# A second pair of input tiles issued ahead of four small parameter loads, and two tiles turned before the parameters' rows

## The reference, cut to what matters

```python
h = rms_norm(x, mix_norm)                  # x * rsqrt(mean(x*x) + 1e-6) * mix_norm
proj = h @ w_in                            # 1024 x 1184
c_q, c_kv, k_pe, u_ssm, conv_a, conv_g = split(proj)
# three mixers: latent attention, a diagonal state-space model (S5), a gated convolution
dt = exp(log_dt); lam_bar = exp((lam_re + 1j * lam_im) * dt)     # parameters of the S5 mixer
x = x + concat(norm(y_attn), norm(y_ssm), norm(y_conv)) @ w_out
x = x + mixture_of_experts(rms_norm(x, ffn_norm))                # 32 experts, two for each token
```

## Time and profile before

| | us |
|---|---|
| runs without a profile, median of 3 | 1185.68 (1184.81 to 1186.89) |
| the profiled execution, its own time | 1187.53 |
| span of that execution in the trace | 1185.8 |
| TensorE busy | 1125.4 (95% of the span) |
| VectorE busy | 978.6 (83%) |
| ScalarE busy | 704.8 (59%) |
| GpSimd busy | 359.7 (30%) |
| mean DMA rate | 220 GB/s |

### The profile page before, as it was taken

How to read it: one execution, slowest core, us unless ns; L and a number is a source line. 1 busy time by engine, 2 the same in 40 slices (tenths; PEclk the granted TensorE clock), 3 DMA queues, 4 the chain that set the end, 5 groups by cost and what they waited for, 6 DMA issues and landing times.

```text
span 1185.8 us, 16012 instructions
## 1 busy us (share of the span) xinstructions
PE 1125.4 (95%) x5762; PEld 873.7 (74%) x5762; DVE 978.6 (83%) x1205; ACT 704.8 (59%) x825; POOL 359.7 (30%) x350
## 2 busy tenths in 40 slices
PE   5999999789999799998899999999999999999996
PEld 3457465666676577888788888888888888888885
DVE  5999989766657654367999999999999999999993
ACT  6521226755466541223577777777777777777772
POOL 4231012379970000112222333323333223223321
PEclk9999999899999899998999999999999999999998
DMA  8300010000005012236999999999999999999962
GB/s 278 111 1 1 1 25 5 1 1 2 2 20 230 1 36 75 86 128 239 382 369 374 374 396 385 389 399 382 395 383 386 389 367 371 393 375 370 397 231 55
DMA packets 40840, 260.96 MB, mean 220 GB/s; under 512 B 16366, under 2 KB 17114, under 8 KB 26970
## 3 DMA queue, kind: packets, MB, share of 16 engines
q1 hardware_dynamic: 30698, 243.03, 52.2%
q0 software_dynamic: 10096, 17.34, 6.0%
HBM read 252.26 MB, written 26.35 MB: 235 GB/s over the span
## 4 chain that ended last, share of the span: by engine, by line
PE 82%; DVE 10%; ACT 3%; issue 3%; DMA 1%; POOL 0%; POOLq 0%; SPq 0%; DVEq 0%; ACTq 0%
PE psum L2243 31%; PE psum L2263 15%; PE psum L1852 8%; PE psum L2151 7%; PE psum L2061 4%; PE psum L2091 3%; DVE arena L1144 3%; PE psum L1905 3%; PE psum L2233 2%; PE psum L2079 2%; PE psum L2249 1%; DVE am L1498 1%; DVE w_rest L1673 1%; PE psum L2047 1%; DMA arena<-in_x 1%
## 5 line engine op out<-in xcount | busy, mean ns | idle before, releaser
L1673 DVE TENSOR_TENSOR w_rest<-w,w_high 128x2048 fp32r<-128x2048 f32 x136 | 305.2, 2286 | 18.7 <-ACT w_high L1056 17.0
L1056 ACT ACTIVATE w_high<-w 128x2048 fp32r<-128x2048 f32 x136 | 256.2, 1913 | 45.4 <-PE psum L2243 42.0
L2243 PE MATMUL psum<-w_high,xgT_high 128*128 128x512 f32 x544 | 216.1, 397 | 3.0 <-DVE xgT_rest L1718 3.0
L2243 PE MATMUL psum<-w_rest,xgT_high 128*128 128x512 f32 x544 | 213.4, 392 | 0.0
L2243 PE MATMUL psum<-w_high,xgT_rest 128*128 128x512 f32 x544 | 212.7, 391 | 0.0
L1725 DVE TENSOR_TENSOR w_rest<-w,w_high 128x2048 fp32r<-128x2048 f32 x66 | 148.1, 2286 | 0.0
L691 POOL DMA_INDIRECT out<-arena,idx x34 | 91.3, 2687 | 106.8 <-DVE arena L1738 101.4
L1066 ACT ACTIVATE w_high<-w 128x2048 fp32r<-128x2048 f32 x66 | 122.4, 1906 | 0.0
L2243 PEld LDWEIGHTS psum<-w_high,xgT_high 128*128 128x128 f32 x544 | 102.7, 189 | 23.7 <-issue 2.2
L2243 PEld LDWEIGHTS psum<-w_rest,xgT_high 128*128 128x128 f32 x544 | 102.5, 188 | 22.0
L2243 PEld LDWEIGHTS psum<-w_high,xgT_rest 128*128 128x128 f32 x544 | 102.7, 189 | 20.5
(11 more groups left out here) (303 smaller groups left out, 2055.2 us busy)
## 6 DMA issues: line engine op xcount, KB each, us to landing
w<-in_w SPq DMA_DIRECT2D x102, 2048.0 KB, 10.3
arena<-in_x SPq DMA_DIRECT2D x5, 1024.0 KB, 9.2
h_scratch<-arena SPq DMA_DIRECT2D x8, 512.0 KB, 2.7
out<-arena SPq DMA_DIRECT2D x8, 512.0 KB, 3.6
arena<-in_x SPq DMA_DIRECT2D x1, 3072.0 KB, 19.1
arena<-in_w_in SPq DMA_DIRECT2D x1, 2688.0 KB, 12.1
arena<-in_w_in SPq DMA_DIRECT2D x1, 2048.0 KB, 13.8
wout_y_raw<-in_w_out SPq DMA_DIRECT2D x1, 2048.0 KB, 7.9
```

Of the source, the lines that this page charges most:

```text
L1056: act.activation(w13h[k][:, c, :], w13[b][k][:, c, :], ACT.Copy).then_inc(W13H_READY[k], 1)
L1673: dve.tensor_tensor(w13l[b][k][:, c, :], w13[b][k][:, c, :], w13h[k][:, c, :].bitcast(F32), S_).then_inc(W13_SPLIT[k], 1)
L2243: last = pe.matmul(psum[:, k, :], x_[:, c, :], w_[:, c, :], start=(c == 0 and n == 0), stop=(c == KC - 1 and n == 2))
```

## The change

On SP's queue `load_x(1)` moves ahead of the four small loads. On VectorE `scale_x(0)` and `scale_x(1)` move ahead of the wait for the transposed parameters and of the two copies; the short steps keep their order, and `scale_x(2)` and `scale_x(3)` keep their places among them. On TensorE `turn_x` takes the tiles' range instead of a half, tiles 0 and 1 are turned before the wait for the four small loads, and tiles 2 and 3 after the parameters' transpose. The number of instructions, their shapes, and the buffers stay as they are.

```diff
@@ SP
             load_x(0)
+            load_x(1)
             for k, lam in enumerate((lam_re, lam_im)):
                 sp.dma_start(first_rows[k * NPAIR:(k + 1) * NPAIR, :], lam[0].rearrange("(r h) s -> r (h s)", h=2)).then_inc(first_rows_in, 16)
...
                 sp.dma_start(ldt.rearrange("p r h -> p (r h)"), log_dt[0].partition_broadcast(P)).then_inc(first_rows_in, 16)
-            load_x(1)
@@ VectorE
+            scale_x(0)
+            scale_x(1)
             dve.wait_ge(hi_filled, R_P1 + 1)
             link(dve.tensor_copy(lamc[:, 0:2, :], psum[:, 5, 0:2 * NPAIR].rearrange("p (k r) -> p k r", k=2)))
             link(dve.tensor_copy(normc[:, 0:KC], psum[:, 5, 2 * NPAIR:2 * NPAIR + KC]))
             dve.sem_inc(hi_drained, 1)
             lr, li = lamc[:, 0, :], lamc[:, 1, :]
-            scale_x(0)
             for h in range(2):
                 ts(v(0)[h * S:(h + 1) * S, :], ldt[h * S:(h + 1) * S, :, h], 1.0 / 16, None, M_)
             ts(v(1), v(0), 1.0 / 9, 1.0, M_, A_)
-            scale_x(1)
             exp_terms(8, 6)
             scale_x(2)
@@ TensorE
-            def turn_x(half):
-                for i in range(4 * half, 4 * half + 4):
+            def turn_x(i0, i1):
+                for i in range(i0, i1):
...
+            turn_x(0, 2)
             pe.wait_ge(first_rows_in, 16 * 4)
             n = 2 * NPAIR + KC
             pe.transpose(psum[:, 5, 0:n], first_rows[:, :], ident[0:n, 0:n]).then_inc(hi_filled, 1)
...
             for half in range(2):
-                turn_x(half)
+                turn_x(4 * half + (0, 2)[half == 0], 4 * half + 4)
```

## The result

| | kernel before | changed kernel |
|---|---|---|
| median of 16 runs, us | 1185.16 (1183.30 to 1186.89) | 1187.59 (1184.79 to 1191.89) |
| profiled execution, its own time | 1187.53 | 1188.29 |
| its span | 1185.8 | 1186.5 |

The ratio is 1.0021 (95% interval 1.0013 to 1.0028): the change costs 2.4 us, 0.21%. The forecast was 1186.4 us, 0.7 us above the median of 1185.68 that was known then, and 0.89 for a difference too small to tell. (The ratios in this document are not the quotients of the medians beside them, and lie up to 0.0013 from these.)

A forecast was written before the change was run, and what follows sets the result against it. The prediction took TensorE's chain through the first projection's start at 18.79 as the bound. Terms of -0.14 (queue and VectorE's list) and +0.84 (clock) made +0.7 on a median of 1185.68: 1186.4 us, range 1183.8 to 1187.6.

The forecast's parts named there:

- What bounds the kernel: TensorE's chain: whatever moves the first projection's start at 18.79 moves the end by the same amount.
- Second pair at 8.11: SP's queue: x's second pair of tiles, loaded ahead of the small loads, lands at 8.11 instead of 11.91.
- The small loads' stall of 3.80 us carried over unchanged: SP's queue: the four small loads land 3.80 us behind x's second pair, at 11.91 instead of 9.51.
- the first rival: Small loads' stall shrinks behind x's second pair: half gives 1184.0 us, chance 0.10; gone gives 1183.1, chance 0.05.
- Tiles 0 and 1 hidden: TensorE's 16 transposes of tiles 0 and 1 end near 12.1, in idle time, as the parameters land.
- -0.14: VectorE's list: starting at 12.22, it begins scale_x(3) at 15.97, 0.14 us earlier than 16.11.
- The clock: TensorE: a 3 us gap ahead of tile 2 leaves the lower clock level, so its transposes take 421 ns.
- +0.84: The clock's share of the forecast on TensorE: 0.84 us later.
- The upper bound: TensorE: clock low until 5 us after 15.33, first 0.7 us of matmuls at half rate, +1.3 us in all.
- The chance of 0.05 for slower: Whole kernel: chance 0.05 of being slower by over 0.2% (2.4 us).
- Order without effect: Rival on SP's queue: the stall belongs to the time, not the loads; 1186.6 us, chance 0.06.
- stall grown: Rival on SP's queue: the small loads' stall grows; at 6 us it gives 1188.6 us, chance 0.05.

The follow-up runs named there:

- t7_tiles_first: Opening alone of the changed kernel with the parameters' transpose after tile 0 and scale_x(2) ahead of the parameters' copies: median 51.14 us.
- e9_tiles_first: t7_tiles_first uncut, as a whole kernel, against the kernel before: 1182.38 us, ratio 0.9972.
- e3_gap_filled: The changed kernel with 16 transposes of the identity in TensorE's gap after the parameters' transpose, against the kernel before: 1187.59 us, ratio 1.0024.
- e1_swap_only: The kernel before with only SP's load order changed, VectorE and TensorE as before: 1185.81 us against 1185.00, ratio 1.0013.
- the ruler: A kernel's opening alone, every engine cut off once the first half's projections are saved; for the kernel before, median 53.27 us.
- t2_after: Opening alone of the changed kernel: 54.52 to 54.70 us in three executions, 56.56 to 56.92 in five, against 53.27 for the kernel before.
- t4_orders: Opening alone of the kernel before with only VectorE's and TensorE's orders changed: 54.62 and 54.75 us, and 56.54 to 57.32 in four executions.
- t3_swap: Opening alone of the kernel before with only SP's load order changed: median 53.62 us against 53.27.
- t8_tiles_first_warm: t7_tiles_first with 24 transposes of the identity ahead of tile 0 on TensorE: median 52.67 us.

## Why the prediction was wrong, point by point

**What bounds the kernel: right.** The first projection's start, and its speed, is what counts. t7_tiles_first and e9_tiles_first show it in the other direction. The one exception is e3_gap_filled, whose later loss stays open.

**Second pair at 8.11: right** (8.31).

**The small loads' stall of 3.80 us carried over unchanged: wrong.** It was 1.9 us behind the second pair in e1_swap_only, and w_in, forecast to land when it did, came 1.8 us earlier in the changed kernel. This is what the first rival said (chance 0.10 for a part of it), which gave 1184.0. The gain did not come, because of the next point. A constant price for these four loads is refuted. The rule that the prediction took from the Trainium skill (DMA: Bandwidth & Descriptors, Anatomy of one DMA: a fixed part that is mostly completion latency, beside the queue) isn't borne out by either number, 3.8 or 1.9 us by which the next load came later; the section describes loads issued by GpSimd, and these are issued by SP.

**Tiles 0 and 1 hidden: the step that failed first in order of time.** Their 16 transposes were forecast to end at 12.1 "just as the parameters land", and ended at 12.39. In e1_swap_only, with the same load order, the parameters were there at 10.17. Since TensorE keeps its order, the transposes set VectorE's first copy: 12.72, not 12.22. The term "-0.14" was +0.45 in the profile (16.56 against 16.11), +0.43 by the ruler. Two ends that meet in a forecast are a wait for whichever comes later. I should have named the parameters' transpose as what is queued behind the tiles, with the price of 2.2 us (12.39 less 10.17) if the loads came sooner. Both prices of the first rival left it out: its list at 10.3, or 9.75, could not start before 16 transposes were done, so 1184.0 and 1183.1 could not be reached by an earlier landing at all.

**The clock: right mechanism, mis-sized term, and the larger part of the miss.** The gap (3.20 us, forecast 3), the 421 ns, and the low level at its end came as forecast. The +0.84, with bounds up to 1.3 for all, should have been 0.9 or 3.0, in the mean 2.2. Of the 2.0 us between the forecast's +0.7 and the ruler's +2.7, 1.4 are this term and 0.6 the one above. For the whole kernel this size is not confirmed, since e3_gap_filled did not win it back. The upper bound was that the clock rises at the latest 5 us after work resumes, from the one rise seen in the opening of before; it rose 8 us after in the profiles of the changed kernel and of t2_after, whose value 5 of 8 executions have. The bound also took half rate for 0.7 us of matmuls; it was 3.5. The section of the Trainium skill named in the prediction (TensorE: Matmul & The Clock Gate, HAM oscillation) describes a burst, a wait for DMA, and a next burst that starts at the low clock. The trace of t4_orders agrees (0.50 from 16.2 on, after 3.21 us of idle time), but for the wait, which is one for VectorE. In the changed kernel's own profile no rise ahead of the gap is to be seen, and the case is another: the clock stayed low across it.

**The range and the chances.** 1187.59 lies at the upper edge of the range, but that is luck: the range was counted from 1185.68, up to +1.9 us, and against the 1185.16 of 16 runs the change costs +2.4. The ratio's interval excludes no change. The chance of 0.05 for slower came from the stall alone. With the clock as a two-valued term of 0.9 or 3.0 I would now put it near one half.

**Order without effect, stall grown: did not occur.** e1_swap_only and t3_swap show the load order doing what it says.

## What to carry to other kernels

When work is moved ahead of a wait on an engine that keeps its order, ask two things: what stands behind that wait and who needs it (here the 24-row transpose on which all of VectorE's list hangs), and what the engine does between the moved work and the next (here nothing, with the clock as the price). Work that was slow but unbroken can be cheaper than the same work done early in two bursts. Measure a change of a few us in an opening by cutting the program off behind it: on the ruler five runs told 0.35 us apart, while the whole kernel's intervals are 1.8 us wide and more. And measure the whole kernel too: one version here lost in it what the opening had won.

## What the runs showed of the hardware that was not expected

The price of four small loads of 20 KB depends on their place: 3.8 us between the first and the second pair of x, 1.9 us between the second pair and w_in, on the same queue. Whether the neighbours make the difference or the moment, no run separates. A clock that is high did not stay so by itself: in t8_tiles_first_warm it fell for 3.3 us of the projection after a wait of 1.9 us, while after 0.9 us in t7_tiles_first it did not. The profiles show one execution of each, but all five times of either kernel lie within 0.4 us of each other. And 24 transposes of the identity ahead of all work, which cost nothing where they stand, made the opening 1.5 us longer.
